# Feed-forward layers: modulation chunks in two halves on GpSimd's own DMA queue and in buffers of their own

## The reference

```python
    cond = jax.nn.silu(c)
    for l in range(DEPTH):
        mod = (cond @ w_ada[l] + b_ada[l]).astype(x.dtype)[:, None, :]
        sh1, sc1, g1, sh2, sc2, g2 = jnp.split(mod, N_MOD, axis=-1)
        h = _rmsnorm(x, norm1_w[l]) * (1.0 + sc1) + sh1
        x = x + g1 * _token_mixers(h, ...)
        h = _rmsnorm(x, norm2_w[l]) * (1.0 + sc2) + sh2
        x = x + g2 * _conv_ffn(h, w_up[l], conv_f_w[l], w_down[l])

def _conv_ffn(h, w_up, conv_w, w_down):
    u = h @ w_up.astype(h.dtype)
    u = _depthwise_conv(u, conv_w)
    gate, val = jnp.split(u, 2, axis=-1)
    return (jax.nn.gelu(gate, approximate=False) * val) @ w_down.astype(h.dtype)
```

## Time and profile before

| | |
|---|---|
| median of 3 runs | 2942.14 us (2940.41 to 2946.04) |
| profiled execution, its own time | 2948.59 us |
| its span, first to last instruction | 2946.8 us |
| TensorE busy | 2781.2 us (94%) |
| VectorE busy | 1617.3 us (55%) |
| ScalarE busy | 1093.0 us (37%) |
| GpSimd busy | 613.0 us (21%) |
| TensorE's share of the chain that ended last | 83% |
| mean granted TensorE clock | 0.974 |

### The profile page before, as it was taken

The page is one execution under the profiler, slowest core; times in us unless marked ns, Lnnn a source line. Parts: engine busy times, 40 slices in busy tenths (PEclk is TensorE's granted clock), DMA queues, the critical chain, the costliest instruction groups (busy, mean ns, idle before and its releaser), DMA issues.

```text
span 2946.8 us, 36236 instructions
## 1 busy us (share of the span) xinstructions
PE 2781.2 (94%) x14816; PEld 2151.1 (73%) x14816; DVE 1617.3 (55%) x2752; ACT 1093.0 (37%) x1788; POOL 613.0 (21%) x338
## 2 busy tenths in 40 slices
PE   6899889999999998999998999989998999989998
PEld 5777568878878676888886877657666878756676
DVE  5779655555567674655456557634425147634324
ACT  2233633322233453433324552243323472244312
POOL 0000025776600001365440231000110131000110
PEclk8899989999999999999999999999999999999999
DMA  7353024454522212344433422121223212121222
GB/s 225 106 163 100 28 86 143 143 172 145 162 85 70 65 42 72 129 143 143 143 115 101 132 87 93 57 65 44 87 71 100 76 44 86 65 65 35 75 87 76
DMA packets 301509, 289.23 MB, mean 98 GB/s; under 512 B 7200, under 2 KB 298144, under 8 KB 301344
## 3 DMA queue, kind: packets, MB, share of 16 engines
q1 hardware_dynamic: 300096, 280.94, 30.0%
q0 software_dynamic: 960, 5.51, 0.5%
q10 hardware_dynamic: 288, 0.47, 0.0%
HBM read 284.80 MB, written 2.10 MB: 97 GB/s over the span
## 4 chain that ended last, share of the span: by engine, by line
PE 83%; DVE 6%; ACT 5%; POOL 2%; DMA 2%; issue 1%; DVEq 0%; SPq 0%; ACTq 0%; POOLq 0%
PE ps L517 81%; PE ps L700 1%; DVE wl L1273 1%; DMA raw<-in_w_in 1%; POOL raw L1741 1%; ACT wh L864 1%; POOL raw L1744 1%; DVE hl L1279 1%; DMA raw<-in_w_up 1%; DVE uv L1279 1%; ACT s L864 0%; POOL ug L1714 0%; DVE adaacc L1279 0%; ACT recat L864 0%; DVE rawt L1279 0%
## 5 line engine op out<-in xcount | busy, mean ns | idle before, releaser
L517 PE MATMUL ps<-hh,wh 128*128 128x512 f32 x2288 | 938.5, 410 | 39.8 <-DVE hl L1279 26.5
L517 PE MATMUL ps<-hh,wl 128*128 128x512 f32 x2288 | 903.6, 395 | 0.0
L517 PE MATMUL ps<-hl,wh 128*128 128x512 f32 x2288 | 903.5, 395 | 0.0
L1273 DVE TENSOR_TENSOR wl<-raw,wh 128x2048 fp32r<-128x2048 f32 (+2 forms) x186 | 448.0, 2409 | 358.8 <-ACT wh L864 358.4
L517 PEld LDWEIGHTS ps<-hh,wh 128*128 128x128 f32 x2288 | 435.8, 190 | 179.2 <-issue 63.6
L517 PEld LDWEIGHTS ps<-hh,wl 128*128 128x128 f32 x2288 | 435.6, 190 | 96.6
L517 PEld LDWEIGHTS ps<-hl,wh 128*128 128x128 f32 x2288 | 436.6, 191 | 87.7 <-issue 5.0
L864 ACT ACTIVATE wh<-raw 128x2048 fp32r<-128x2048 f32 (+2 forms) x186 | 342.5, 1841 | 255.4 <-PE ps L517 145.2
L1741 POOL TENSOR_TENSOR raw<-raw,cond 128x2048 f32<-128x2048 f32 x40 | 180.3, 4507 | 244.2 <-DMA raw<-in_w_ada 244.2
L864 ACT ACTIVATE rawt<-ps 128x512 f32<-128x512 f32 (+1 forms) x106 | 63.3, 597 | 319.3 <-PE ps L517 318.9
L1744 POOL TENSOR_TENSOR raw<-raw 128x1024 f32<-128x1024 f32 x80 | 172.3, 2154 | 6.3
(11 more groups left out here) (231 smaller groups left out, 3859.9 us busy)
## 6 DMA issues: line engine op xcount, KB each, us to landing
raw<-in_w_in SPq DMA_DIRECT2D x74, 1024.0 KB, 5.3
raw<-in_w_ada SPq DMA_DIRECT2D x64, 1024.0 KB, 5.3
raw<-in_w_up SPq DMA_DIRECT2D x44, 1024.0 KB, 5.2
raw<-in_w_in SPq DMA_DIRECT2D x44, 512.0 KB, 5.1
raw<-in_w_out SPq DMA_DIRECT2D x16, 1024.0 KB, 5.5
raw<-in_w_down SPq DMA_DIRECT2D x16, 1024.0 KB, 5.3
stage<-in_w_ada SPq DMA_DIRECT2D x8, 1024.0 KB, 11.4
raw<-in_w_down SPq DMA_DIRECT2D x8, 768.0 KB, 4.7
```

The lines of the kernel that those rows point to most:

```text
L517: return e.matmul(o, a, b, start=start, stop=stop, skip_group_check=True)
L1273: return e.tensor_tensor(o, a, b, op)
```

## The change

In the feed-forward layers the third raw buffer is given up. In its place, of the same size, come two buffers `strewn0` and `strewn1` of 128 x 4 x 256. Chunks there no longer pass through SyncE: GpSimd issues the transfer of each half of a chunk from its own queue, the half of the next chunk as soon as it has used the buffer. The weights keep `raw0` and `raw1` to themselves. Each half is multiplied and added up alone, which makes seven instructions and two DMA issues per chunk in place of four instructions. The wait for the end of attention moves from SyncE to GpSimd, once per layer. The wait for the accumulator's former sums moves to the first half. The order of units is the same.

```diff
-        self.raw.append(sb(f"raw{NR}", [128, 2048]))
+        self.strewn = [sb(f"strewn{i}", [128, 4, 256])[:, :, :] for i in range(2)]
...
+    def ada_load(j, h):
+        go.wait_ge(*last("pool_ada"))
+        e.dma_start(M.strewn[h], plan[j]["srcs"][0][:, 4 * h:4 * h + 4, :]).then_inc(*X.tally.up16(f"strewn_in{h}", ("strewn", j, h)))
...
     def ada(j):
-        go.wait_ge(*at("raw", j))
         go.wait_ge(*at("small", "cond"))
-        e.tensor_tensor(v, v, weights, ALU.mult).then_inc(*up("pool_ada"))
-        for k in (4, 2):
-            go.wait_ge(*last("pool_ada"))
-            e.tensor_tensor(v[:, 0:k, :], v[:, 0:k, :], v[:, k:2 * k, :], ALU.add).then_inc(*up("pool_ada"))
...
+        if p["first"]:
+            go.wait_ge(*at("s3", "1", p["layer"], 2, 3))
+            for h in range(2):
+                ada_load(j, h)
+        for h in range(2):
+            v = M.strewn[h]
+            go.wait_ge(*at("strewn", j, h))
+            e.tensor_tensor(v, v, weights, ALU.mult).then_inc(*up("pool_ada"))
+            go.wait_ge(*last("pool_ada"))
+            e.tensor_tensor(v[:, 0:2, :], v[:, 0:2, :], v[:, 2:4, :], ALU.add).then_inc(*up("pool_ada"))
+            go.wait_ge(*last("pool_ada"))
+            if h == 0:
+                if X.acc_before[p["chunk"]] is not None:
+                    go.wait_ge(*at("sums", X.acc_before[p["chunk"]]))
+                e.tensor_tensor(acc[:, :], v[:, 0, :], v[:, 1, :], ALU.add).then_inc(*up("pool_ada"))
+            else:
+                e.tensor_tensor(v[:, 0, :], v[:, 0, :], v[:, 1, :], ALU.add).then_inc(*up("pool_ada"))
+                go.wait_ge(*last("pool_ada"))
+                e.tensor_tensor(acc[:, :], acc[:, :], v[:, 0, :], ALU.add).then_inc(*up("pool_ada", ("acc", p["chunk"])))
+            if p["next"] is not None:
+                ada_load(p["next"], h)
...
     for j, p in enumerate(plan):
+        if p["strewn"]:
+            continue
...
-        if p["after_attention"] is not None:
-            go.wait_ge(*at("s3", "1", p["after_attention"], 2, 3))
...
-        p["slot"] = i = min(range(NR + 1 if long_ else NR), key=lambda i: -1 if raw_in[i] is None else raw_in[i])
+        else:
+            p["slot"] = i = min(range(NR), key=lambda i: -1 if raw_in[i] is None else raw_in[i])
```

More of the change, by code:

```diff
@@ L1731, in c_low @@
             e.tensor_tensor(low, sticks(M, c, u, b)[0], high.bitcast(F32), ALU.subtract).then_inc(*up("pool_c", ("c_low", l, c, u)))
+    def ada_load(j, h):
+        go.wait_ge(*last("pool_ada"))
+        e.dma_start(M.strewn[h], plan[j]["srcs"][0][:, 4 * h:4 * h + 4, :]).then_inc(*X.tally.up16(f"strewn_in{h}", ("strewn", j, h)))
     def ada(j):
         p = plan[j]
-        acc, v = M.adaacc[X.acc[p["chunk"]]], M.piece(M.raw[p["slot"]], p, 0)
+        acc = M.adaacc[X.acc[p["chunk"]]]
         c0 = 0 if p["chunk"][0] == 1 else 8
-        go.wait_ge(*at("raw", j))
@@ L1739, in ada @@
         go.wait_ge(*at("small", "cond"))
-        weights = M.cond[:, c0:c0 + KD].rearrange("p (k n) -> p k n", n=1).broadcast_to([128, KD, 256])
-        e.tensor_tensor(v, v, weights, ALU.mult).then_inc(*up("pool_ada"))
-        for k in (4, 2):
-            go.wait_ge(*last("pool_ada"))
-            e.tensor_tensor(v[:, 0:k, :], v[:, 0:k, :], v[:, k:2 * k, :], ALU.add).then_inc(*up("pool_ada"))
-        go.wait_ge(*last("pool_ada"))
-        if X.acc_before[p["chunk"]] is not None:
-            go.wait_ge(*at("sums", X.acc_before[p["chunk"]]))
@@ L1748, in ada @@
-        e.tensor_tensor(acc[:, :], v[:, 0, :], v[:, 1, :], ALU.add).then_inc(*up("pool_ada", ("acc", p["chunk"])))
+        if p["first"]:
[4 more added lines that the diff above has]
+            v = M.strewn[h]
+            weights = M.cond[:, c0 + 4 * h:c0 + 4 * h + 4].rearrange("p (k n) -> p k n", n=1).broadcast_to([128, 4, 256])
+            go.wait_ge(*at("strewn", j, h))
+            e.tensor_tensor(v, v, weights, ALU.mult).then_inc(*up("pool_ada"))
+            go.wait_ge(*last("pool_ada"))
+            e.tensor_tensor(v[:, 0:2, :], v[:, 0:2, :], v[:, 2:4, :], ALU.add).then_inc(*up("pool_ada"))
[10 more added lines that the diff above has]
+                ada_load(p["next"], h)
@@ L1813, in prepared @@
     splits = 0
-    raw_in, layer, long_ = [None] * (NR + 1), None, False
+    raw_in, layer, long_, strewn = [None] * NR, None, False, None
     for j, p in enumerate(plan):
@@ L1818, in prepared @@
             layer = p["key"][1] if long_ and not was else layer
-        p["long"] = long_
-        p["slot"] = i = min(range(NR + 1 if long_ else NR), key=lambda i: -1 if raw_in[i] is None else raw_in[i])
-        p["raw_before"], raw_in[i] = raw_in[i], j
-        p["after_attention"] = layer if i == NR and (p["raw_before"] is None or plan[p["raw_before"]]["after_attention"] != layer) else None
+        p["long"], p["strewn"] = long_, long_ and p["kind"] == "ada"
+        if p["strewn"]:
+            p["layer"], p["next"] = layer, None
+            if strewn and strewn["layer"] == layer:
+                strewn["next"] = j
+            p["first"] = not (strewn and strewn["layer"] == layer)
+            strewn = p
+        else:
+            p["slot"] = i = min(range(NR), key=lambda i: -1 if raw_in[i] is None else raw_in[i])
+            p["raw_before"], raw_in[i] = raw_in[i], j
         off, p["views"], p["loads"], p["srcs"] = 0, [], [], [src for _, _, src in p["pieces"]]
```

## The result

| | before | after |
|---|---|---|
| median, us | 2941.43 (4 runs, 2940.41 to 2946.04) | 2962.04 (4 runs, 2957.44 to 2968.29) |
| ratio, 95% interval | | 1.0067, 1.005 to 1.0084 |
| profiled execution, own time, us | 2948.59 | 2960.71 |
| its span, us | 2946.8 | 2958.9 |
| TensorE busy, us | 2781.2 | 2781.8 |

The change costs 20.6 us in the median (by the interval 14.7 to 24.7). That is slower by more than a run's resolution. It lies inside the range that was given, near its slow end, and 12 us above the end of what the likeliest case was to give (2936 to 2950).

What follows compares the result with a forecast made beforehand. TensorE, busy 94% of the span, was taken to bound the kernel. New waits (+8.0, +4.1), savings (-3.0, -4.1, -0.8) and clock (-1.6, +2.1) summed to +4.7 us on the median 2942.14: 2946.5 us, range 2931 to 2966.

Steps and rivals of the forecast that it cites:

- the likeliest case: Whole kernel: an issue takes 0.55 to 1.0 us, new TensorE waits replace old; 2936 to 2950 us, chance 50%.
- The chunk on GpSimd: Feed-forward chunk on GpSimd: seven instructions take 9.3 us plus two issues of 0.9 each, 11.1 us alone.
- channels 20 and 21: First layer, two chunks before the last channel pair: TensorE waits 5.9 us instead of 1.84, +4.1 us.
- three waits for 1.87 each: First layer, three places with two chunks in a row: TensorE waits 4.5 us instead of 1.87, together +8.0 us.
- norm: Ahead of the first layer: opening chunks start earlier, so the norm's last addition and matmuls are no longer slowed, -3.0 us.
- 637.68 and 650.02: First-layer TensorE waits: shorter GpSimd multiplications and earlier low parts save 1.3 us at 637.68; the buffer wait at 650.02 saves 0.8.
- second layer: Waits at 1372.59 and 1485.51, VectorE waiting for GpSimd, go as halves shorten the multiplications: -2.8 us.
- clock: Slow TensorE matmuls after waits: -1.6 us from old waits gone, +2.1 from four new waits paying in the same proportion.
- the lock: Behind GpSimd's gating, VectorE's low part waits up to 1.89 us more if GpSimd has just begun a multiplication.
- issues go by rows or late landings: GpSimd's issues cost by row, 2.2 us each, or transfers land late: 2950 to 2975 us, chance 27%.
- GpSimd keeps up: VectorE and GpSimd slip past each other, issues take 0.55 us, no new wait comes: 2925 to 2936 us, chance 18%.
- The own queue changes nothing: GpSimd's separate queue doesn't help, the 1.87 us waits stay: 2942 us, chance 5%.

Runs made afterwards that it cites:

- The reorder of `fs`: Changed kernel, with copy and small subtraction of a gated channel moved behind the next weights' split (even channels and last pair): 2933.15 us; the kernel before, likewise reordered: 2943.48 us.
- the settings: GpSimd memsets of an unread buffer ahead of each half, added to the kernel whose SyncE issues the halves: one per half 2944.01 us, two 2973.88 us.
- the kernel with one setting: Kernel whose SyncE issues the halves, plus one GpSimd memset of 128 x 1024 into an unread buffer ahead of each half: 2944.01 us.
- the kernel with two settings: Kernel whose SyncE issues the halves, plus two GpSimd memsets into an unread buffer ahead of each half: 2973.88 us.
- the first experiment: Changed kernel, but SyncE issues the halves and puts the second of two neighbouring chunks off until the next weight load is issued: 2927.08 us.

## Why the prediction was right or wrong

**The chunk on GpSimd** was right. The second chunk of the pair, undisturbed, takes 490.77 to 501.93, 11.16 us (said: 11.1). One issue is 0.79 us, not the 0.9 taken, but idle time ahead of it is 0.30, not 0.08; together that is nearly the same (1.09 for 0.98). So part of this hit is two errors that cancel. The block of two was to be 26.8 us at d = 0.79 (d is the time of one issue) and is 26.7.

**Where TensorE would wait and for whom** was right: one load behind the old wait, which is what its sum reckons with (516.2), and behind channels 20 and 21, ended by VectorE behind ScalarE behind GpSimd. Only the names are one pair off: the weights are those of channels 6 and 7, 10 and 11, 14 and 15; 4 and 5, 8 and 9, 12 and 13 are the channels whose gating holds them up. The reorder of `fs` shows that the link is its place in the order of ScalarE and VectorE (2933.15), the settings that the source is GpSimd's time. The old 1.87 us waits, for a buffer, are gone, as said; that weights need only two buffers held too: ScalarE waited for feed-forward weight transfers in before and nowhere in the first layer of after.

**What was mis-sized**, term by term of the sum (us):

| term | predicted | measured |
|---|---|---|
| three waits for 1.87 each | +8.0 | +10.7 (16.3 - 5.6) |
| channels 20 and 21 | +4.1 | +4.4 (6.21 - 1.84) |
| wait at 710.20 | 0 | +1.7 |
| norm | -3.0 | -3.0 |
| 637.68 and 650.02 | -2.1 | -2.1 |
| second layer | -2.8 | -3.1 |
| clock | -1.6 + 2.1 | +7.0 |
| sum | +4.7 | +15.6 |

(By whole layers it was 15.2; the wait of 0.23 us at 753.79, which is gone too, is in no term.)

The largest miss is the clock. The prediction let four new waits pay in the same proportion as the old ones, one in three. But the old ones were 1.87 us long and the new ones 5 to 6, and of those each one paid: the 48 matmuls behind them take 13.21, 13.82, 13.02 and 13.85 us, where 11.14 is the time at 1.00. That is 9.3, less the 1.6 that before had lost; the layer's busy time as a whole grew by 7.0. The waits of 2.86 and 3.13 us in the kernel with one setting paid each time too, 12.5 to 12.8 us for 48 matmuls. A wait costs more than its length here. The trace of before had a row for a long wait, though not between busy stretches: the layer's first 48 matmuls, after a wait of 3.98 us and 10.5 us in which TensorE was busy for 3.5, took 13.90 us at a clock of 0.79. The prediction priced by the short waits alone. The windows, of the kernel with one setting at 512.47, then of before:

```profile
512.47:525.07 12.60, 12.60 (x49) 10.30 (x50) 8.66 (x9) 2.94 (x4) 10.88 (x8) 0.88 0.49 158
```

```profile
434.79:448.69 13.90, 13.90 (x49) 11.23 (x50) 10.85 (x14) 6.78 (x8) 0.00 (x0) 0.79 0.04 10
```

The second is the lock: VectorE and GpSimd waiting for each other's instructions. The prediction had one wait for it behind the gating, 0 to 1.9 us on 6.22. The 6.22 us are exactly what the kernel with two settings takes, by the path of the sum (copy, high part, low part). After takes 8.37, 2.15 more, just past the upper bound, and by another path: ScalarE's high part is done at 505.73, but VectorE's small subtraction, which loses twice, at 506.91, and the low part behind it takes 3.29 us instead of 2.29.

The third is the late landing: at 549.29 the second half of a chunk waited 1.09 us for its transfer, which took 6.98 us from the issue to the landing where the median of after is 4.2; such a wait was said to cost up to one. TensorE's wait of that place is 6.11, the other two are 5.08.

```profile
549.29 1.88 POOL L1752 TENSOR_TENSOR strewn<-strewn,cond 128x1024 f32<-128x1024 f32 x1 [1.09 <-DMA strewn<-in_w_ada]
```

The fourth is the wait of 1.66 us at 710.20, after five chunks in the first down-projection. The prediction had it only in the rival, for d = 2.2; at d = 0.79 it was there already.

That the time still lies in the stated range is in part luck. Its slow end was set for issues of 1.5 us with clock and lock at their worst; the issues took 0.79, and clock and lock used up the room.

**The rivals.** The time came out where "issues go by rows or late landings" was to end (2950 to 2975), but not by that rival: 512 rows cost 0.20 us more than 128, not four times as much. "GpSimd keeps up" fell with the first long wait: the two engines did not slip past each other, and that rival's time (2925) was nearly reached only by the kernel whose SyncE issues the chunks (2927.08). "The own queue changes nothing" fell with the places of the waits.

**What stays open**: some 5 us between the two layers of the traces and the medians; and which of VectorE and GpSimd comes first when both want to go on, which came out one way in after and the other in the first experiment. That two settings per half bring shorter waits than expected because of it is read from VectorE's rows, not tried by itself.

## What to carry to other kernels

A transfer that is moved to a compute engine's queue pays there for its issue and for the pause ahead of it, and every instruction of that engine's and of its readers' streams that stands behind pays with it; follow the first such reader to TensorE before moving anything (here ScalarE's copy and VectorE's subtraction, the unit `fs`). Look at the order on an in-order queue before adding buffers or queues: putting the second of two neighbouring chunks off behind one weight load was worth 29 us, and moving the unit `fs` behind the next split 29 as well. Price a long TensorE wait with the slower matmuls that follow it, from rows that show a wait of that length; here the start of the layer had one.

## What the runs showed of the hardware

- An issue on GpSimd took 0.59, 0.79 and 0.92 us for 128, 512 and 1024 rows of the same 512 KB; when it waits for the instruction just ahead, the engine idles 0.30 us first, where the next arithmetic instruction starts after some 0.07.
- A VectorE instruction that has to wait for GpSimd's can lose again to the next one: 0.68 us of work took 2.95 us. The Trainium skill (SBUF — State Buffer, Who interferes with whom) calls the pair of ports that the two engines share an exclusive lock. The trace agrees, and shows that the one who waited isn't always served first: in after GpSimd's second gating multiplication ended at 504.5 and its next multiplication, started at 504.46, still came ahead of VectorE. In the first experiment, at the same place, VectorE came first (1.10 us) and the multiplication took 2.34; what decides is open. Settings of a buffer on GpSimd did not hold VectorE up (1.08 and 2.29 us beside them).
- After TensorE waits of 5.08 to 6.21 us the granted clock was 0.78 to 0.85 over the next 13 us, after those of 2.86 and 3.13 us in the kernel with one setting 0.87 or 0.88 over the next 12.5 to 12.8; after 1.66 us it was 1.00. Of the two levels, 1.2 and 2.4 GHz, part of that stretch ran at the lower, for 1.9 to 2.7 us more after each of the long waits.
